# One encoder kernel, three edits: keys scaled by ScalarE, an identity added by VectorE, Y corrected first

## The reference

```python
proj = x @ W_in                                   # q, k, v, z, beta, decay, windowed q/k/v, gates
q, k, v = silu(conv5(proj[qkv]))                  # 8 heads of 128; q and k are L2-normed
# gated delta rule, once forwards and once backwards, per head:
T = inverse(I + strict(beta * (k k^T) * decay))   # block of 128 tokens here
state = state * exp(g) + k_dec^T (T (v - k state))
o_dn = rms_norm(o_fwd + o_bwd) * silu(z)
o_sw = softmax(q k^T / 8 within +-128 tokens, with a sink) @ v       # 16 heads of 64, 4 key heads
x = layer_norm(alpha * x + (gate_a * (o_dn @ W_A) + gate_b * (o_sw @ W_B)) @ W_out)
x = layer_norm(alpha * x + (silu(x @ W_g) * (x @ W_u)) @ W_d)
```

## Time and profile before

| what | value |
|---|---|
| median of 3 runs | 2342.47 us (2341.98 to 2345.06) |
| the profiled execution | 2347.63 us, span 2345.8 us |
| PE busy | 2261.1 us, 96% of the span |
| DVE, ACT, POOL busy | 47%, 36%, 49% |
| mean granted PE clock | 0.987 of full speed |
| chain that ended last | PE 86%, DVE 9%, issue 2%, ACT 2%, DMA 1% |

### The profile page before, as it was taken

How to read it: one execution, slowest core, us unless ns; L and a number is a source line. 1 busy time by engine, 2 the same in 40 slices (tenths; PEclk the granted TensorE clock), 3 DMA queues, 4 the chain that set the end, 5 groups by cost and what they waited for, 6 DMA issues and landing times.

```text
span 2345.8 us, 34138 instructions
## 1 busy us (share of the span) xinstructions
PE 2261.1 (96%) x13464; PEld 1823.5 (78%) x13464; DVE 1113.9 (47%) x1948; ACT 833.2 (36%) x2220; POOL 1142.9 (49%) x674
## 2 busy tenths in 40 slices
PE   8999999999999899999999999999899999999997
PEld 6777877877777788888777778778677787888885
DVE  4677677764444611110256776777544466111003
ACT  3555445466641211110135454444665403111100
POOL 5453333324337466666544442332343375666664
PEclk9999999999999999999999999999999999999998
DMA  4221111111124223322222211211111332322322
GB/s 152 72 81 48 48 57 57 43 50 46 55 79 143 75 91 98 99 92 97 92 99 72 81 47 41 64 51 51 41 55 55 108 108 90 99 92 97 117 90 81
DMA packets 53886, 182.64 MB, mean 78 GB/s; under 512 B 7520, under 2 KB 8160, under 8 KB 53728
## 3 DMA queue, kind: packets, MB, share of 16 engines
q1 hardware_dynamic: 48976, 167.01, 22.1%
q10 hardware_dynamic: 4752, 13.45, 1.6%
HBM read 169.94 MB, written 4.19 MB: 74 GB/s over the span
## 4 chain that ended last, share of the span: by engine, by line
PE 86%; DVE 9%; issue 2%; ACT 2%; DMA 1%; POOL 0%; DVEq 0%; ACTq 0%; POOLq 0%
PE PS L586 19%; PE PS L588 18%; PE PS L587 18%; PE PS L754 11%; PE PS L844 2%; PE PS L958 2%; PE PS L1025 2%; PE PS L830 2%; PE PS L972 1%; PE PS L848 1%; PE PS L903 1%; PE PS L887 1%; PE PS L781 1%; PE PS L894 1%; PE PS L924 1%
## 5 line engine op out<-in xcount | busy, mean ns | idle before, releaser
L547 POOL TENSOR_SCALAR wh<-w_raw 128x1024 fp32r<-128x1024 f32 (+1 forms) x255 | 277.1, 1087 | 1029.5 <-DMA w_raw<-stream 1028.6
L550 POOL TENSOR_TENSOR wl<-w_raw,wh 128x1024 fp32r<-128x1024 f32 (+1 forms) x255 | 615.5, 2414 | 21.3
L586 PE MATMUL PS<-xh,wh 128*128 128x512 f32 x992 | 398.2, 401 | 11.1 <-issue 6.1
L588 PE MATMUL PS<-xl,wh 128*128 128x512 f32 x992 | 390.3, 393 | 0.0
L587 PE MATMUL PS<-xh,wl 128*128 128x512 f32 x992 | 389.2, 392 | 0.0
L586 PEld LDWEIGHTS PS<-xh,wh 128*128 128x128 f32 x992 | 188.2, 190 | 57.3 <-issue 12.7
L588 PEld LDWEIGHTS PS<-xl,wh 128*128 128x128 f32 x992 | 187.7, 189 | 40.6
L587 PEld LDWEIGHTS PS<-xh,wl 128*128 128x128 f32 x992 | 188.6, 190 | 37.4
L754 PE MATMUL PS<-xh,wh 128*128 128x512 f32 x448 | 205.3, 458 | 5.1 <-DVEq L1692 3.4
L2000 DVE TENSOR_TENSOR hf<-sg,PS 128x512 f32<-128x512 f32 x44 | 30.3, 688 | 355.5 <-PE PS L588 355.5
L1645 DVE SCALAR_TENSOR_TENSOR conv_acc<-PS,cw,conv_acc 128x510 f32<-128x510 f32 x192 | 143.9, 749 | 105.3 <-ACT conv_acc L1187 99.8
(11 more groups left out here) (293 smaller groups left out, 4779.3 us busy)
## 6 DMA issues: line engine op xcount, KB each, us to landing
w_raw<-stream SPq DMA_DIRECT2D x254, 512.0 KB, 3.4
w_raw_spare<-stream SPq DMA_DIRECT2D x46, 512.0 KB, 3.5
x<-x_in ACTq DMA_DIRECT2D x6, 512.0 KB, 7.0
qx<-qx SPq DMA_DIRECT2D x48, 64.0 KB, 2.0
raw<-raw SPq DMA_DIRECT2D x32, 64.0 KB, 2.2
ln_g<-ln_rows ACTq DMA_DIRECT2D x4, 512.0 KB, 4.0
ln_b<-ln_rows ACTq DMA_DIRECT2D x4, 512.0 KB, 5.0
x_park<-x ACTq DMA_DIRECT2D x4, 512.0 KB, 5.0
```

What stands on the lines that cost most here:

```text
L547: nc.gpsimd.tensor_scalar(wh[s][:, w], w_raw[s][:, w], 1.0, 1.0, ALU.mult, ALU.mult).then_inc(w_hi_done, 1)
L550: nc.gpsimd.tensor_tensor(wl[s][:, w], w_raw[s][:, w], wh[s][:, w].bitcast(F32), ALU.subtract).then_inc(split_done, 1)
L586: mm(o, ah, bh, start=first, stop=False)
L588: return mm(o, ah, bl, start=False, stop=last)
```

## The change

There are five edits, for both layers.

1. **Keys.** The scaling of the keys (`kn = raw * rn`) moves from DVE (one instruction of 128x512 in `front_scale`) to ACT (`scale_keys`: four instructions of 128x128). For the next head they stand after levels 3 and 5. For head 0 of a layer they stand in ACT's iteration `i = 10`, ahead of `front_turned`.
2. **Factors.** The buffer `ht` and its copy (L1581) are dropped; the factors are read from `tab`.
3. **Identity.** PE no longer writes the identity ahead of L858; DVE reads the sum out of PSUM and computes `sum * 1024 + 1024 * I` into `V` in one instruction. ACT's scaling (L1288) goes.
4. **Order on DVE.** `V` and `YF` come first after level 6, then the scaled keys, then the copies of `fill_out`.
5. **Scores.** The queries meet all their two or three blocks of keys in one matmul of 256 or 384 columns.

```diff
                     for r in range(2):
                         pe.wait_ge(y_upd[r], n * 7 + 7)
-                        mm(PS[:, 3 * r, :].rearrange("p (c t) -> p c t", c=CHUNKS), id_16[:], rows(id_16[:]), start=True,
-                           stop=False, skip_group_check=True)
                         for c in range(CHUNKS):
                             o = PS[:, 3 * r, c * P:(c + 1) * P]
-                            mm(o, NAh[r][:, c, :], Y[r][:, c, :], start=False, stop=False, skip_group_check=True)
-                            ins = mm(o, NAl[r][:, c, :], Y[r][:, c, :], start=False, stop=True,
-                                     skip_group_check=True)
+                            mm(o, NAh[r][:, c, :], Y[r][:, c, :], start=True, stop=False)
+                            ins = mm(o, NAl[r][:, c, :], Y[r][:, c, :], start=False, stop=True)
                         ins.then_inc(e_mm[r], 1)
...
                     for t in range(2):
-                        for j in range(hi - lo):
-                            for half in range(2):
-                                part = slice(half * HD, (half + 1) * HD)
-                                mm(PS[:, half * 2 + t, j * P:(j + 1) * P], qx[part, g * 2 + t, b * P:(b + 1) * P],
-                                   kz[part, g, (lo + j) * P:(lo + j + 1) * P], start=j == 0, stop=lo + j == b,
-                                   skip_group_check=True)
+                        for half in range(2):
+                            part = slice(half * HD, (half + 1) * HD)
+                            mm(PS[:, half * 2 + t, 0:(hi - lo) * P], qx[part, g * 2 + t, b * P:(b + 1) * P],
+                               kz[part, g, lo * P:hi * P], start=True, stop=False, skip_group_check=True)
...
+                def scale_keys(h, t, chunks):
+                    for c in chunks:
+                        ins = A(kn[t][:, c, :], raw[:, h + HEADS, c, :], ACT.Copy, scale=rn[:, h + HEADS, c:c + 1])
+                    if c == CHUNKS - 1:
+                        ins.then_inc(k_normed, 1)
...
                     if i == 10:
+                        act.wait_ge(gate_dve, l * 19 + 19)
+                        scale_keys(0, 0, range(CHUNKS))
                         front_turned(l * HEADS, 0)
...
+                        if more and lev in (3, 5):
+                            scale_keys(h + 1, 1 - s, (0, 1) if lev == 3 else (2, 3))
...
-                    for r in range(2):
-                        act.wait_ge(e_mm[r], n + 1)
-                        A(V[r][:].rearrange("p c t -> p (c t)"), PS[:, 3 * r, :], ACT.Copy,
-                          scale=E_SCALE).then_inc(e_ready[r], 1)
...
-            nc.vector.tensor_copy(id_16[:], ident).then_inc(ready_bf, 1)
+            TS(id_e[:], ident, E_SCALE, None, ALU.mult).then_inc(ready_bf, 1)
...
-                def front_scale(h, m, t):
-                    nc.vector.tensor_copy(ht[t][:].rearrange("p k r c -> p (k r c)"),
-                                          tab[:, bass.ds(h, 1)].rearrange("p a k r c -> p (a k r c)")).then_inc(head_cols, 1)
-                    TT(kn[t][:], raw[:, h + HEADS, :, :], cols(rn[:, h + HEADS, :]), ALU.mult).then_inc(k_normed, 1)
...
                     if i == 9:
                         key_scales()
-                        front_scale(0, m0, 0)
...
-                    if more:
-                        front_scale(h + 1, n + 1, 1 - s)
-                    fill_out(ISSUED[h, "L6"])
-                    scaled_keys(n, s)
+                    for r in range(2):
+                        dve.wait_ge(e_mm[r], n + 1)
+                        STT(V[r][:], bank(3 * r), E_SCALE, rows(id_e[:]), ALU.mult, ALU.add).then_inc(e_ready[r], 1)
                     for r in range(2):
                         dve.wait_ge(y_fix[r], n + 1)
                         STT(YF[r][:], bank(3 * r), 1.0 / E_SCALE, Y[r][:], ALU.mult, ALU.add).then_inc(y_done[r], 1)
+                    scaled_keys(n, s)
+                    fill_out(ISSUED[h, "L6"])
```

More of the change, by code:

```diff
@@ L172, in trunk @@
         id_bf = place("id_bf", [P, P], BF16)
-        id_16 = place("id_16", [P, P], F16)
+        id_e = place("id_e", [P, P], F16)
         minus_id = place("minus_id", [P, P], F32)
@@ L245, in trunk @@
         OT = [head_buf(f"OT{r}", [P, P]) for r in range(2)]
-        ht = [head_buf(f"ht{s}", [P, 5, 2, CHUNKS]) for s in range(2)]
         egl = [[head_buf(f"egl{s}{r}", [P, CHUNKS]) for r in range(2)] for s in range(2)]
@@ L361, in trunk @@
         gate_act = sem("gate_act")
-        head_cols = sem("head_cols")
         k_normed = sem("k_normed")
@@ L1221, in front_decays @@
                             ins = A(DT[r][:, c, :], PS[:, 4 + r, c * P:(c + 1) * P], ACT.Exp,
-                                    bias=ht[t][:, T_NEG_CUM, r, c:c + 1])
+                                    bias=tab[:, m % HEADS, T_NEG_CUM, r, c:c + 1])
                         ins.then_inc(decay_done, 1)
@@ L1308, in head @@
                                 A(O1[r][:], PS[:, 2 + r, 0:P], ACT.Copy,
-                                  scale=ht[s][:, T_EG, r, c:c + 1]).then_inc(o1_ready[r], 1)
+                                  scale=tab[:, h, T_EG, r, c:c + 1]).then_inc(o1_ready[r], 1)
                         if step == 1:
@@ L1578, in bank @@
                     return PS[:, b, :].rearrange("p (c t) -> p c t", c=CHUNKS)
-                def front_scale(h, m, t):
-                    nc.vector.tensor_copy(ht[t][:].rearrange("p k r c -> p (k r c)"),
-                                          tab[:, bass.ds(h, 1)].rearrange("p a k r c -> p (a k r c)")).then_inc(head_cols, 1)
-                    TT(kn[t][:], raw[:, h + HEADS, :, :], cols(rn[:, h + HEADS, :]), ALU.mult).then_inc(k_normed, 1)
                 def front_beta(m, t, r):
                     dve.wait_ge(decay_done, m * 2 + r + 1)
-                    TT(TMP[r][:], DT[r][:], cols(ht[t][:, T_NEG_BETA, r, :]), ALU.mult).then_inc(beta_decay, 1)
+                    TT(TMP[r][:], DT[r][:], cols(tab[:, m % HEADS, T_NEG_BETA, r, :]), ALU.mult).then_inc(beta_decay, 1)
                 def front_nat(m, t, r):
@@ L1627, in scaled_keys, with edge_scales @@
                         TT(to, kn[t][:, of, :], cols(bdl[r][:, of]), ALU.mult).then_inc(kb_ready[r], 1)
-                def edge_scales(t):
+                def edge_scales(h):
                     for r in range(2):
                         edge = P - 1 if r == 0 else 0
-                        TT(bdl[r][:], DT[r][:, :, edge], ht[t][:, T_BETA, r, :], ALU.mult).then_inc(bdl_done, 1)
+                        TT(bdl[r][:], DT[r][:, :, edge], tab[:, h, T_BETA, r, :], ALU.mult).then_inc(bdl_done, 1)
                 def conv_pair(i, sides=(0, 1)):
@@ L1744, in head @@
                         if lev == 4:
-                            edge_scales(s)
+                            edge_scales(h)
                         if lev in (3, 5):
@@ L1769, in head @@
                                 dve.wait_ge(ks_mm[r], n * 3 + step)
-                                STT(R[r][:], PS[:, r, 0:P], ht[s][:, T_NEG_EG, r, c:c + 1], value(c), ALU.mult,
+                                STT(R[r][:], PS[:, r, 0:P], tab[:, h, T_NEG_EG, r, c:c + 1], value(c), ALU.mult,
                                     ALU.add).then_inc(r_ready[r], 1)
```

## The result

The changed kernel takes 2354.12 us (median of 6 runs, 2353.86 to 2354.84). The kernel before, in six runs of the same comparison, takes 2345.55 us; three more runs had come to the three shown above, at 2347.00, 2348.28 and 2346.04. The ratio is 1.0041, interval [1.0031, 1.0052]: slower, by 9.6 us by the ratio and 8.6 by the two medians. The two profiled executions stand at 2347.63 and 2353.86 us, +6.2.

What follows compares the result with a forecast made beforehand. PE, busy for 96% of the span, was taken to bound the kernel. +10.9 + 3.3 - 7.0 + 0 - 3.3 + 2.4 - 1.4 = +4.9 us on the median of 2342.47 gave 2347 us, range 2342 to 2352.

Steps and rivals of the forecast that it cites:

- Slower: Whole kernel: a time above the upper line of 2347.2 us, 0.2% over the median; chance 0.50.
- The waits at the key turn: Turn of head 0's keys, each layer: PE idles for ACT's late scaling, 5.5 and 5.4 us, together +10.9 us.
- The clock: Behind PE's wait for head 0's keys: 3.3 us at half clock, one stretch in each layer, +3.3 us.
- The identity: Correction of Y, 16 heads: PE drops 32 identity matmuls of 0.22 us, -7.0 us, with V still in time.
- YF ahead of the keys: DVE after level 6: with YF before kb and kn, PE's three waits for YF go, -3.3 us.
- kn late at head 3: Head 3, both layers: DVE's kn, held up by POOL's subtraction, comes 1.2 us late twice, +2.4 us.
- The scores: Attention scores, 16 blocks of each kind in two layers: fewer, longer matmuls save PE -1.4 us.
- The sum on the profiled run: Whole kernel: all terms give +4.9 us, taking the profiled span from 2345.8 us and the execution's 2347.63 us to 2352.5 us.
- The part without the late keys: Terms besides head 0's key wait and its clock: identity -7.0, YF -3.3, kn +2.4, scores -1.4 us.
- The late keys: Turn of head 0's keys, both layers: idle waits of +10.9 us and slow clock of +3.3 us.
- The base and the size: Whole kernel: the difference of +4.9 us put on the median of 2342.47 us, giving 2347.4 us.

Runs made afterwards that it cites:

- keys early: The changed kernel with ACT scaling head 0's keys ahead of the first SiLU of iteration i = 10, not behind the second; 2337.17 us, ratio 0.9961.
- the wait was filled: The changed kernel with 21 matmuls of 128x512, their result unread, on PE ahead of the turn of head 0's keys; 2352.67 us, ratio 1.0034.
- keys half-way: The changed kernel with head 0's keys scaled behind the copy of the second unit, ahead of its SiLU; 2345.64 us, ratio 1.0005.
- only the keys: The kernel before with only the key scaling moved to ACT and factors read from tab; identity, order and scores as before; 2359.14 us, ratio 1.0062.
- the last experiments: The kernel before and the changed kernel, each with X masked from PSUM instead of SBUF; 2345.54 us and 2354.28 us.

## Why the prediction was right in sign and wrong in size

Forecast was 2347 us with 2342 to 2352 as the range; it is 2354.12. "Slower" had 0.50, and the waits that made it slower are the ones named. In short, two steps failed: the base, a median of three that was 3.1 us too low, and the size of the difference, +4.9 forecast for 8.6 measured, in which the clock behind the key turn was the term found undersized. Step by step:

- **The waits at the key turn: right.** 10.9 us forecast, 10.6 measured, by the mechanism named: ACT behind SiLU behind DVE's taps. It can be hidden, and wasn't, by the position alone, as "keys early" shows.
- **The clock: undersized.** "One in each layer: +3.3 us" from a stretch of 3.3 us each. Measured 4.7 and 4.5 us of work at 0.50, and 2.2 us back in each layer when the wait was filled: 4.4 us, and 5.6 against "keys early". The row that I took was behind a wait of 2.17 us; at 2.0 us ("keys half-way") it is again 3.4 us. Behind 5.3 us the clock falls during the wait already and the stretch is 6.8 us long (156.7 to 163.5), of which work takes 4.7. By the rule of the Trainium skill that I quoted (TensorE: Matmul & The Clock Gate, section HAM oscillation — how this bites in real kernels), the next group starts cold; the trace agrees here, for the turn itself took 1.12 us where it takes 0.60 in the earlier trace rows, while in the earlier trace rows the first matmul was still at full speed.
- **The identity: right.** In the changed kernel and in "keys early" PE never waits for `V` ahead of the product with `X`. The cleanest comparison is with "only the keys", from which the changed kernel differs by the identity, the order on DVE and the scores: of the twelve segments from E to E, head 3's left out, nine are 0.2 to 0.6 us shorter (0.44 forecast) and three 0.9 to 1.8.
- **YF ahead of the keys: size right, cause incomplete.** The 3.3 us of waits are gone. "Only the keys" shows that they go already with DVE's copy of `ht` and the scaling, which I had costed at nothing. With `V` on DVE, which I had costed at nothing too, the old order brings 14.8 us of them (in "keys early"); the new order prevents that, which is worth 11.6 us by the spans and more by the ratios.
- **kn late at head 3: right.** +2.4 forecast, waits of 3.1 us in the changed kernel and 2.8 in "keys early", once in each layer at head 3, beside POOL's subtraction; with `kb` and `kn` on ACT they are gone.
- **The scores:** -1.4 forecast, -1.1 measured.
- **The sum on the profiled run: near, and in part by luck.** It gave 2352.5; measured is 2353.86, +6.2 for +4.9. But the profiled execution of the kernel before stood 2.1 us above the median of six; by the medians the difference is 8.6. The part without the late keys was -9.3 us in the forecast (-7.0, -3.3, +2.4, -1.4); "keys early" has -9.5 by the spans. The late keys were +14.2; the spans of the changed kernel and "keys early" differ by 15.8, their medians by 17.0. The meeting of `X` with POOL at head 4 of layer 1 (+4.9 in that segment) was in no term; the others happened to make up for it in this trace.
- **The base and the size: the steps that failed.** "The same difference on the median gives 2347.4 us" started from 2342.47, the median of three. These three were low ones. The next three were 2346.0 to 2348.3, the median of six is 2345.55, and the 21 runs beside the last experiments go from 2341.35 to 2350.74 with a median of 2346.11. With 2345.55 the same sum gives 2350.5. So of the 6.7 us between 2347.4 and 2354.12, 3.1 are the base and 3.7 are the difference (8.6 for +4.9). Of these 3.7, 1.1 to 2.3 are the clock behind the key turn (4.4 to 5.6 for 3.3) and 0.7 the waits for `kn` (3.1 for 2.4); for the rest the cause stays open, the collision of `X` with POOL at head 4 is the one candidate seen. Counted on the profiled executions the shares are 5.4 us for the transfer to the median and 1.3 for the sum, but this count hands the 2.1 us by which one execution stood above its median to the transfer. A gap of 5.2 us between a profile and a median of three is itself the sign that the kernel varies by as much, and the range should have held 2352.5, the sum on its own execution, well inside and not just outside.

What stays open is why the kernel before varies by 9 us between runs. It isn't the collision of `X` with POOL. It differs between the traces where the short stretches of half clock stand. In all twelve traces they begin during a wait of PE of over 1 us or within 2.5 us behind it, but for the last one of each trace and two others; yet the same wait has one in one trace and none in another. PE ahead of the sums of the decays, first in the changed kernel and then in that with the filled wait, which are the same up to there, each with the window behind it:

```profile
97.14 0.63 PE L715 MATMUL PS<-sm,cst 128*128 128x32 f32 x4 [1.50 <-DVE sm L1523]
98.70:102.10 3.40, 3.40 (x10) 2.63 (x9) 1.98 (x3) 2.25 (x3) 3.22 (x2) 0.50 0.00 0
...
96.86 0.63 PE L715 MATMUL PS<-sm,cst 128*128 128x32 f32 x4 [1.50 <-DVE sm L1525]
98.00:102.00 4.00, 4.00 (x20) 3.26 (x19) 2.37 (x4) 2.69 (x6) 3.36 (x2) 1.00 0.00 0
```

A wait of 1.50 us was followed by half clock once and not the other time; and in the kernel before a wait of 2.45 us ahead of 1167.86 was followed by none, where one of 2.47 ahead of 790.25 was. By my estimate each such stretch of 3.4 us costs 1.7 us if PE has work in it, so a few more or fewer would make the spread. That is argued and not shown: I have no experiment that holds them fixed.

## What to carry to other kernels

When a step moves to another engine, read what stands ahead of it in that engine's order, down to the wait that ends last there: the same four instructions in the same iteration cost 17 us behind a SiLU and nothing 9 us earlier. Free time on an engine is used by whoever is queued next, so look what a removed instruction lets start: without DVE's copy and scaling the `YF` waits were gone even in the old order. And a forecast of an absolute time needs the spread of the kernel before; three runs that agree within 3.1 us said nothing about it here.

## What the runs showed of the hardware

- A wait of PE can cost more than its length. The two of 2.0 us at the key turn and one of 2.17 were followed, 0.9 to 1.5 us after the restart, by 3.4 us at 1.2 GHz; the 5.3 us by a fall while PE still waited, and by 4.5 to 4.7 us of work at 1.2 GHz. But length alone does not decide: waits of 1.50 us stand with and without a fall behind them, and so do waits of 2.45 and 2.47. Matmuls whose result nobody reads kept the clock up at both key turns.
- A DVE instruction with both inputs in SBUF took 0.42 us in the median and 2.62 beside POOL's subtraction (`X`), 0.56 and 2.54 (`kn`). The copy `ht`, with one, took 0.17 and 1.82. The same mask `X` with one input in PSUM took 0.67 to 0.69 us in all 32 places, six of them beside that subtraction. ACT's pieces of `kb` took 0.39 to 0.40 us in all 48.
- 384 columns of scores in one matmul on half of the array instead of three of 128 bring 3% of that step, not more: 1.56 us for eight against 1.61 for 24.
